# Prompt attention: the causal mask added by VectorE, the turn of probabilities as a product with diagonals

## The chip, the cores and the metric

One core of one Trainium2 chip runs the whole kernel. Its engines are TensorE (PE; its weight loads are shown apart as PEld), VectorE (DVE), ScalarE (ACT), GpSimd (POOL) and SyncE (SP), which issues most loads and stores. The metric is the device time of one execution in microseconds, over three runs.

## The reference, cut to what matters

The kernel computes one step of a hybrid decoder layer for a prompt of 512 rows and for 8 sequences of 4 new rows. The part that matters here is the prompt's attention over selected blocks and over the window. With 512 rows there are only 8 blocks and 16 may be chosen, so both branches become ordinary causal attention over 512 rows, each with its own keys and values:

```python
s_s = jnp.einsum('bqgrd,bqgkcd->bqgrkc', q, kb).astype(jnp.float32) * scale
m_s = (pos <= t_q[None, :, None, None, None]) & jnp.isfinite(top_s)[..., None]
p_s = masked_softmax(...)                      # selected branch
s_w = jnp.einsum('bqgrd,bkgd->bqgrk', q, kw).astype(jnp.float32) * scale
m_w = ((diff >= 0) & (diff <= WINDOW) & (t_w >= 0)[None, :])[None, :, None, None, :]
p_w = masked_softmax(s_w, m_w)                 # window branch
return gate[..., 0:1] * o_c + gate[..., 1:2] * o_s + gate[..., 2:3] * o_w
```

There are 2 groups of 6 query heads with 64 numbers each. A row's probabilities are the exponentials over their sum, and each branch's output is scaled by a gate of that row, head and branch.

## The kernel before, in words

The kernel goes through its stages one after the other: input projections, the RWKV scan, a stretch of "fill" projections that run beneath the scan and the compressed attention, then the prompt's attention, the prompt's memory attention, the same for the samples, the merge and the feed-forward part. The order on each engine is written out by hand; engines meet through semaphores. No planner sets the order in the stretch of the change.

Prompt attention is cut into units, `ATT_UNITS`. A unit is (r, t, bs): the query head r of both groups (g = 0, 1), the tile t of 128 query rows, and the branches bs. For t = 0 and 1 both branches fit a unit; for t = 2 and 3 there is one unit for each branch. So a head has 6 units (t = 0, 1, 2, 2, 3, 3), and 6 heads have 36. Only keys up to the tile's end are used, w = (t + 1) x 128 of them, so the mask matters in the last 128 keys alone.

A unit passes these steps:

- `att_scores` (TensorE, L1733): q times keys into the accumulator `acc[u % 2]`, one product per group, in f32 with 64 rows of weights. Then, at L1735, one bf16 product per group of the identity with the causal mask (0 or -1e30) adds the mask to the last 128 keys of each branch. From the third unit on it first waits for the exponentials of the unit two before (`at_exp`). It counts up `at_s`.
- `att_max` (VectorE, L3017) waits for `at_s` and takes the negated maximum over each row.
- `att_exp` (ScalarE, L2396) writes exp(score - maximum) to `probs[u % 3]` and the sums to `small`.
- `att_scale` (VectorE): reciprocal of the sums (L3027), times the gate (L3028), then the probabilities times that factor, in place: one tensor_tensor where a unit has two branches (L3032), one tensor_scalar per group where it has one (L3035). It counts up `at_scaled`.
- `att_turn` (TensorE, L1745) waits for `at_scaled` and transposes each 128x128 block of `probs` into `acc[2]`: 4, 8, 6, 6, 8 and 8 blocks in the six units of a head, 40 in all.
- `att_copy` (ScalarE, L2406) copies them to `probsT`.
- `att_values` (TensorE, L1756) multiplies them with the values into `acc[3]`, with 64 columns of weights per group. After a head, `att_out` (VectorE, L3041) adds the result to `onsaT`.

TensorE's loop is scores(u), turn(u - 2), values(u - 3). VectorE's is max(u), scale(u - 1), and now and then `att_out`. ScalarE's is copy(u - 2), exp(u). `settle()` is a count of TensorE's own semaphore between groups. `own(...)` on VectorE runs an instruction and then waits until it is done.

Behind the 36 units comes the prompt's memory attention, with scores (L1769), transposes of 128x128 blocks (L1796, eight for a query tile) and values (L1809, eight f32 products of 128x128 weights with 128 columns for a query tile).

The buffer that the change adds lies in the region `late_at`, where the fill stretch kept rows on their way to memory; each store counts up a semaphore `spilled`. SyncE waits for all of them before it issues the page keys (L730) of the third pair of samples.

Of the kernel before, what the change touches and what calls it, by code (L numbers as in the profile page):

```python
# [13 lines left out]
P = 128  # L14
# [230 lines left out]
def bc(ap, axis, n):  # L245

    a = ap.unsqueeze(axis)
    shape = list(a.shape)
    shape[axis] = n
    return a.to_broadcast(shape)  # L250
# [17 lines left out]
def program(nc, A):  # L268
    with ExitStack() as ctx:
# [21 lines left out]
        def region(start, *shape):  # L291

            if start is None:
                start = at[0]
            n = int(np.prod(shape))
            at[0] = start + n
            assert at[0] <= 35200, at[0]
            ap = work[:, KT * T + start:KT * T + start + n]
            names = "abcd"[:len(shape)]
            if len(shape) == 1:  # L300
                return ap
            return ap.rearrange(f"p ({' '.join(names)}) -> p {' '.join(names)}",
                                **dict(zip(names[1:], shape[1:])))

        def const(name, rows=P):
            lo, hi = SEG[name]
            return cst[0:rows, lo:hi]
# [21 lines left out]
        bf_causal = region(None, P // 2).bitcast(BF16)  # L329
        bf_cmp = region(None, QT * NC_P // 2).bitcast(BF16)  # L330
        late_at = at[0]
        m_probT = [region(None, MEM_H * 2, P) for _ in range(2)]
        assert at[0] <= 16800
        smp1 = 16800
        w1_two = region(smp1 + 7168, 2, CMP // 2, P)
# [699 lines left out]
        def _(pe):  # L1035
# [687 lines left out]
            def att_scores(u):  # L1723
                r, t, bs = ATT_UNITS[u]
                w, nb = (t + 1) * P, len(bs)
                if u >= 2:
                    pe.wait_ge(at_exp, u - 1)
                settle()
                o = acc[u % 2][:, :, 0:nb * w].rearrange("p g (b k) -> p g b k", b=nb)
                for g in range(NG):  # L1730
                    gs = slice(g * HD, (g + 1) * HD)
                    keys = in_all[gs, T_ATT[bs[0]]:T_ATT[bs[-1]] + 1:T_WK - T_SK, 0:w]
                    pe.matmul(o[:, g], qT[gs, r, t * P:w], keys, start=True, stop=False)  # L1733
                for g in range(NG):
                    mm = pe.matmul(o[:, g, :, t * P:w], bf_ident, bc(bf_causal, 1, nb), start=False, stop=True)  # L1735
                mm.then_inc(at_s, 1)

            def att_turn(u):
                r, t, bs = ATT_UNITS[u]
                pe.wait_ge(at_scaled, u + 1)  # L1740
                if u:
                    pe.wait_ge(at_copied, u)
                for g in range(NG):
                    for k in range(len(bs) * (t + 1)):
                        mm = pe.transpose(acc[2][:, g, k * P:(k + 1) * P], probs[u % 3][:, g, k * P:(k + 1) * P], ident)  # L1745
                mm.then_inc(at_turn, 1)

            def att_values(u):
# [844 lines left out]
        def _(dve):  # L2593
# [419 lines left out]
            def att_max(u):  # L3013
                r, t, bs = ATT_UNITS[u]
                w, nb, c = (t + 1) * P, len(bs), 16 * (u % 2)
                dve.wait_ge(at_s, u + 1)
                dve.tensor_reduce(small[:, c:c + 2 * nb].rearrange("p (g b) -> p g b", g=NG),  # L3017
                                  acc[u % 2][:, :, 0:nb * w].rearrange("p g (b k) -> p g b k", b=nb), AX, ALU.max, negate=True)\
                   .then_inc(at_max, 1)

            def att_scale(u):
                r, t, bs = ATT_UNITS[u]
                w, nb, c = (t + 1) * P, len(bs), 16 * (u % 2)
                rows = lambda n: small[:, c + n:c + n + NG * nb]
                gates = gates_tm[:, t, :].rearrange("p (g r b) -> p g r b", g=NG, b=3)[:, :, r, 1 + bs[0]:2 + bs[-1]]
                dve.wait_ge(at_exp, u + 1)
                own(dve.reciprocal(rows(8), rows(4)))  # L3027
                own(dve.tensor_tensor(rows(12).rearrange("p (g b) -> p g b", g=NG),  # L3028
                                      rows(8).rearrange("p (g b) -> p g b", g=NG), gates, ALU.mult))
                if nb == 2:  # L3030
                    shown = probs[u % 3][:, :, 0:nb * w].rearrange("p g (b k) -> p g b k", b=nb)
                    ins = dve.tensor_tensor(shown, shown, bc(rows(12).rearrange("p (g b) -> p g b", g=NG), 3, w), ALU.mult)  # L3032
                else:
                    for g in range(NG):
                        ins = dve.tensor_scalar(probs[u % 3][:, g, 0:w], probs[u % 3][:, g, 0:w],  # L3035
                                                small[:, c + 12 + g:c + 13 + g], None, ALU.mult)
                ins.then_inc(at_scaled, 1)

            def att_out(r):
                dve.wait_ge(at_pv, HEAD_UNITS * (r + 1))  # L3040
# [1 line left out]

            page_copy(0)
            att_max(0)
            for u in range(1, N_ATT + 1):
                if u < N_ATT:
                    att_max(u)
                if u == 1:
                    new_copy(0)
                att_scale(u - 1)  # L3050
                if u >= 5 and (u - 5) % HEAD_UNITS == HEAD_UNITS - 1:
                    att_out((u - 5) // HEAD_UNITS)
# [386 lines left out]
```

## Time and profile before

| | |
|---|---|
| median of 3 runs | 1466.07 us (1464.58 to 1468.4) |
| profiled execution | 1465.81 us, span 1464.1 us, mean granted clock 0.996 |
| TensorE busy | 1430.9 us, 98% of the span |
| VectorE, ScalarE, GpSimd busy | 847.9, 413.0 and 211.9 us |
| prompt attention's first scores | 665.74 us from the start of the span |
| its last values (L1756) start | 775.8 us |

The page gives busy times of the whole span; its ends of matmuls are modelled, so how tightly TensorE is packed is read from starts in the timeline. In a timeline row the numbers are the start and the length in us, then engine, line, operation, the program's names (written from read), the size of the weights, the shape of one operand and the count of merged instructions. In brackets is the idle time before, with its releaser. In a row of windows come: the window, its length, the busy time and count of PE, PEld, DVE, ACT and POOL, the granted clock as a share, the share of the DMA engines and GB/s. In a row of grouped instructions come: busy us in total, mean ns of one, and the idle time before.

### The profile page before, as it was taken

To read this page: it belongs to the slowest core of one execution; us is meant where nothing else is said; L and a number is where in the kernel's file an instruction comes from. 1 tells how busy PE (TensorE), PEld (TensorE's weight loads), DVE (VectorE), ACT (ScalarE), POOL (GpSimd) and SP (SyncE) were. 2 spreads that over 40 slices of the span, in tenths; PEclk is the share of its full clock that TensorE was granted. 3 is DMA by queue.
4 is the path that set the end of the run, shared out by engine and by line. 5 is a ranking of instruction groups with operands and counts; after the bars stand their busy time and mean duration, and the time that the engine had idled before them with its cause. 6 is when DMAs were issued, how large, how long until landed. Compare 5 with 4: busy or idle time off the path is not lost.

```text
span 1464.1 us, 30419 instructions
## 1 busy us (share of the span) xinstructions
PE 1430.9 (98%) x12340; PEld 1130.4 (77%) x12340; DVE 847.9 (58%) x1649; ACT 413.0 (28%) x890; POOL 211.9 (14%) x276
## 2 busy tenths in 40 slices
PE   9999999999999999999999889999999999999997
PEld 8887578878888866775667668888888888888886
DVE  7665058633433447526774537677666766666664
ACT  3112372123333316227775631102311011101001
POOL 1000324532222224434001210000000000000000
PEclk9999999999999999999999999999999999999999
DMA  6222543211111238457003963432222222222221
GB/s 264 87 87 72 182 166 111 96 61 44 50 46 36 101 118 254 156 165 250 1 2 91 334 260 137 141 98 83 75 84 86 76 83 87 87 74 97 90 87 61
DMA packets 57399, 163.94 MB, mean 112 GB/s; under 512 B 7312, under 2 KB 19696, under 8 KB 55952
## 3 DMA queue, kind: packets, MB, share of 16 engines
q1 hardware_dynamic: 48608, 121.46, 24.9%
q0 software_dynamic: 7936, 39.40, 7.8%
q8 instruction: 99, 1.62, 0.5%
q10 hardware_dynamic: 720, 1.16, 0.2%
q14 instruction: 36, 0.29, 0.1%
HBM read 144.01 MB, written 22.15 MB: 113 GB/s over the span
## 4 chain that ended last, share of the span: by engine, by line
PE 91%; DVE 4%; ACT 2%; issue 1%; SPq 1%; DMA 1%; DVEq 0%; ACTq 0%
PE acc L1059 26%; PE acc L1210 17%; PE acc L1978 5%; PE acc L2006 5%; PE acc L1987 5%; PE acc L2031 4%; PE acc L1152 2%; PE acc L1332 2%; PE acc L1167 2%; PE acc L1733 2%; PE acc L1745 2%; PE acc L1756 1%; PE acc L1349 1%; PE acc L1094 1%; PE acc L1071 1%
## 5 line engine op out<-in xcount | busy, mean ns | idle before, releaser
L1059 PE MATMUL acc<-sb_work,sb_ring 128*128 128x272 f32 x602 | 150.9, 392 | 0.0
L2524 ACT ACTIVATE sb_omemT<-acc 128x272 f32<-128x272 f32 x74 | 29.3, 396 | 386.0 <-PE acc L1978 234.2
L1210 PE MATMUL acc<-sb_work,sb_ring 128*128 128x272 f32 x504 | 129.2, 398 | 4.4 <-DVE sb_work L2733 2.9
L1059 PE MATMUL acc<-sb_work 128*128 128x272 f32 x530 | 133.0, 393 | 0.0
L1059 PEld LDWEIGHTS acc<-sb_work,sb_ring 128*128 128x128 f32 x602 | 114.4, 190 | 23.6
L1059 PEld LDWEIGHTS acc<-sb_work 128*128 128x128 f32 x530 | 100.5, 190 | 21.4 <-issue 0.8
L1210 PEld LDWEIGHTS acc<-sb_work,sb_ring 128*128 128x128 f32 x504 | 93.1, 190 | 25.7 <-issue 7.1
L1978 PE MATMUL acc<-sb_work,sb_ring 128*128 128x272 f32 x308 | 77.2, 393 | 1.0 <-issue 1.0
L1987 PE MATMUL acc<-sb_work,sb_ring 128*128 128x272 f32 x308 | 77.1, 392 | 0.0
L1210 PE MATMUL acc<-sb_onsaT,sb_omemT 128*128 128x272 f32 x272 | 69.5, 399 | 0.0
L1978 PEld LDWEIGHTS acc<-sb_work,sb_ring 128*128 128x128 f32 x308 | 58.4, 190 | 13.4 <-issue 1.4
L1987 PEld LDWEIGHTS acc<-sb_work,sb_ring 128*128 128x128 f32 x308 | 58.5, 190 | 12.1
L1059 PE MATMUL acc<-sb_onsaT,sb_work 128*128 128x272 f32 x266 | 66.6, 393 | 0.0
L1059 PE MATMUL acc<-sb_onsaT,sb_ring 128*128 128x272 f32 x266 | 66.5, 392 | 0.0
L1210 PEld LDWEIGHTS acc<-sb_onsaT,sb_omemT 128*128 128x128 f32 x272 | 50.2, 190 | 13.3 <-issue 3.2
L1059 PEld LDWEIGHTS acc<-sb_onsaT,sb_work 128*128 128x128 f32 x266 | 50.4, 190 | 10.6 <-issue 0.2
L1059 PEld LDWEIGHTS acc<-sb_onsaT,sb_ring 128*128 128x128 f32 x266 | 50.5, 190 | 10.4
L2830 DVE TENSOR_TENSOR sb_work<-acc,sb_cst 128x192 f32<-128x192 f32 x64 | 22.7, 358 | 55.8 <-PE acc L1332 55.5
L1210 PE MATMUL acc<-sb_work,sb_omemT 128*128 128x272 f32 x208 | 53.8, 399 | 0.0
L3017 DVE TENSOR_REDUCE sb_small<-acc 128x2 f32<-128x768 f32 (+3 forms) x36 | 37.7, 1047 | 20.4 <-PE acc L1735 19.6
L844 POOL TENSOR_TENSOR sb_omemT<-sb_ring 128x512 f32<-128x512 f32 x20 | 26.1, 1304 | 148.7 <-PE acc L1210 100.8
L1210 PEld LDWEIGHTS acc<-sb_work,sb_omemT 128*128 128x128 f32 x208 | 38.3, 190 | 9.8 <-issue 1.2
(495 smaller groups left out, 2787.4 us busy)
## 6 DMA issues: line engine op xcount, KB each, us to landing
sb_ring<-w_stream SPq DMA_DIRECT2D x144, 512.0 KB, 3.5
sb_work<-pages SPq DMA_DIRECT2D x56, 192.0 KB, 4.2
branch_gates<-sb_work SPq DMA_DIRECT2D x24, 272.0 KB, 2.8
sb_work<-branch_gates POOLq DMA_DIRECT2D x8, 816.0 KB, 14.7
sb_ring<-w_stream SPq DMA_DIRECT2D x16, 384.0 KB, 3.3
sb_work<-mem_kT SPq DMA_DIRECT2D x8, 512.0 KB, 7.5
sb_work<-mem_v SPq DMA_DIRECT2D x8, 512.0 KB, 9.9
query_features<-sb_work SPq DMA_DIRECT2D x10, 272.0 KB, 3.5
```

What stands on the lines that cost most here:

```text
L1059: mm = pe.matmul(out, w[:, q, :], x[q], start=q == 0, stop=q == n - 1)
L1152: mm = pe.matmul(acc[n][:, h, :], memT[:, k, n * P:(n + 1) * P], w[:, 4 * h:4 * h + 4, :].rearrange("p a c -> p (a c)"), start=k == 0, sto ...
L1167: mm = pe.matmul(acc[a][:, b, 0:HALF_T], lhsT, rhs[:, b * HALF_T:(b + 1) * HALF_T], start=True, stop=True)
L1210: mm = pe.matmul(acc[3][:, (7 * u + ph) % 2, 0:HALF_T], w, x, start=q == 0 and ph in (0, 1, 5), stop=q == 3, skip_group_check=True)
L1332: mm = pe.matmul(acc[1][rows[1 - e], s, k * C:k * C + n], gram[rows[e], par, e, 3 * s + k, n:2 * n], X(par, 3 * s + k)[rows[e], 0:n], star ...
L1733: pe.matmul(o[:, g], qT[gs, r, t * P:w], keys, start=True, stop=False)
L1978: mm = pe.matmul(bank(u, 0), w[:, 2 * q, :], x[:, x0 + 2 * q, LO], start=q == 0, stop=q == n - 1)
L1987: mm = pe.matmul(bank(u, 1), w[:, 2 * q + 1, :], x[:, x0 + 2 * q + 1, LO], start=q == 0, stop=q == n - 1)
L2006: mm = pe.matmul(bank(u, 3), s1[:, q, :], sums[:, 0, q], start=q == 0, stop=q == n - 1)
L2031: mm = pe.matmul(acc[out][:, b, 0:HALF_T], w[:, k, :], sources[g][:, k, b * HALF_T:(b + 1) * HALF_T], start=k == 0, stop=k == MERGE_KS[g] - 1)
L2524: act.activation(keeps(u)[:, s], bank(u, (0, 3)[s]), ACT.Copy).then_inc(unit_kept, 1)
L3017: dve.tensor_reduce(small[:, c:c + 2 * nb].rearrange("p (g b) -> p g b", g=NG), acc[u % 2][:, :, 0:nb * w].rearrange("p g (b k) -> p g b k ...
```

## The change

Three things are changed.

1. `att_scores` no longer adds the mask. `att_max` does it on VectorE: one tensor_tensor per unit adds the f32 constant "causal" to the last 128 keys of each group and branch, in place in the accumulator, and waits for its own end before the maximum.
2. `att_scale` no longer scales the probabilities. It builds, for each group and branch, a 128x128 diagonal matrix: the identity times the factor gate over sum of each row (`scale_diag`, three buffers in turn). `att_turn` multiplies each block of raw exponentials with that diagonal instead of transposing it against the identity. A block as weights times a diagonal gives the transposed block with its columns scaled.
3. `scale_diag` gets the place of the two `m_probT` buffers, which now lie over it, and VectorE waits, after the first unit's maximum, for all `spilled` counts.

```diff
@@ buffers
         late_at = at[0]
-        m_probT = [region(None, MEM_H * 2, P) for _ in range(2)]
+        scale_diag = region(late_at, 3, 2 * NG, P)
+        m_probT = [region(late_at + n * MEM_H * 2 * P, MEM_H * 2, P) for n in range(2)]
@@ att_scores
-                    pe.matmul(o[:, g], qT[gs, r, t * P:w], keys, start=True, stop=False)
-                for g in range(NG):
-                    mm = pe.matmul(o[:, g, :, t * P:w], bf_ident, bc(bf_causal, 1, nb), start=False, stop=True)
+                    mm = pe.matmul(o[:, g], qT[gs, r, t * P:w], keys, start=True, stop=True)
                 mm.then_inc(at_s, 1)
@@ att_turn
-                        mm = pe.transpose(acc[2][:, g, k * P:(k + 1) * P], probs[u % 3][:, g, k * P:(k + 1) * P], ident)
+                        mm = pe.matmul(acc[2][:, g, k * P:(k + 1) * P], probs[u % 3][:, g, k * P:(k + 1) * P],
+                                       scale_diag[:, u % 3, g * len(bs) + k // (t + 1), :], start=True, stop=True)
@@ att_max
                 dve.wait_ge(at_s, u + 1)
+                ahead = acc[u % 2][:, :, 0:nb * w].rearrange("p g (b k) -> p g b k", b=nb)[:, :, :, t * P:w]
+                own(dve.tensor_tensor(ahead, ahead, bc(bc(const("causal"), 1, nb), 1, NG), ALU.add))
@@ att_scale
-                if nb == 2:
-                    shown = probs[u % 3][:, :, 0:nb * w].rearrange("p g (b k) -> p g b k", b=nb)
-                    ins = dve.tensor_tensor(shown, shown, bc(rows(12).rearrange("p (g b) -> p g b", g=NG), 3, w), ALU.mult)
-                else:
-                    for g in range(NG):
-                        ins = dve.tensor_scalar(probs[u % 3][:, g, 0:w], probs[u % 3][:, g, 0:w],
-                                                small[:, c + 12 + g:c + 13 + g], None, ALU.mult)
-                ins.then_inc(at_scaled, 1)
+                dve.tensor_tensor(scale_diag[:, u % 3, 0:NG * nb, :], bc(ident, 1, NG * nb), bc(rows(12), 2, P), ALU.mult)\
+                   .then_inc(at_scaled, 1)
@@ VectorE's attention loop
             att_max(0)
+            for n in range(2):
+                dve.wait_ge(spilled[n], 16 * N_FILL // 2)
```

## Rows read from the trace of the kernel before

**Rows 1.** The page: busy time, granted clock in 40 slices, chain that ended last.

```profile
PE 1430.9 (98%) x12340; PEld 1130.4 (77%) x12340; DVE 847.9 (58%) x1649; ACT 413.0 (28%) x890; POOL 211.9 (14%) x276
...
PEclk9999999999999999999999999999999999999999
...
PE 91%; DVE 4%; ACT 2%; issue 1%; SPq 1%; DMA 1%; DVEq 0%; ACTq 0%
```

**Rows 2.** One head in a window: length, busy (count) of five engines, clock, DMA, GB/s.

```profile
680.00:697.29 17.29, 17.17 (x158) 10.98 (x158) 13.49 (x30) 13.33 (x38) 7.16 (x13) 1.00 0.82 254
```

**Rows 3.** Timeline of one head: start, length (us), engine, line, operation, idle before.

```profile
680.00 0.88 PE L1756 MATMUL acc<-sb_work 128*64 128x128 f32 x12
...
680.81 0.70 PE L1733 MATMUL acc<-sb_work 64*128 64x256 f32 x4
...
680.97 0.88 DVE L3035 TENSOR_SCALAR sb_omemT<-sb_omemT,sb_small 128x512 f32<-128x512 f32 x2
...
681.44 0.39 PE L1735 MATMUL acc<-sb_work 128*128 128x256 bf16 x2
...
681.91 0.86 PEld L1745 LDWEIGHTS acc<-sb_cst,sb_omemT 128*128 128x128 f32 x8 [0.35 <-DVE sb_omemT L3035]
...
683.74 1.13 PE L1733 MATMUL acc<-sb_work 64*128 64x512 f32 x4
...
684.81 0.39 PE L1735 MATMUL acc<-sb_work 128*128 128x256 bf16 x2
...
685.03 1.04 PE L1745 MATMUL acc<-sb_cst,sb_work 128*128 128x128 f32 x8
...
685.24 1.23 DVE L3017 TENSOR_REDUCE sb_small<-acc 128x4 f32<-128x1024 f32 x1 [1.48 <-PE acc L1735]
...
686.00 1.10 PE L1756 MATMUL acc<-sb_work 128*64 128x128 f32 x16
...
686.38 0.17 DVE L3027 RECIPROCAL sb_small<-sb_small 128x4 f32<-128x4 f32 x1
...
686.78 0.69 DVE L3032 TENSOR_TENSOR sb_omemT<-sb_omemT,sb_small 128x512 f32<-128x512 f32 x1
...
687.88 0.29 PE L1735 MATMUL acc<-sb_work 128*128 128x128 bf16 x2
...
688.01 0.61 PE L1745 MATMUL acc<-sb_cst,sb_omemT 128*128 128x128 f32 x4
...
688.54 1.10 PE L1756 MATMUL acc<-sb_work 128*64 128x128 f32 x16
...
690.76 0.86 PEld L1745 LDWEIGHTS acc<-sb_cst,sb_omemT 128*128 128x128 f32 x8 [0.22 <-DVE sb_omemT L3032]
```

**Rows 4.** Groups of instructions by shape: the mask matmuls of two-branch units.

```profile
L1735 PE MATMUL acc<-sb_work 128*128 128x256 bf16 x24 | 4.7, 278 | 0.0
```

**Rows 5.** Timeline of TensorE in the memory attention that follows.

```profile
777.79 1.04 PE L1796 MATMUL acc<-sb_cst,sb_work 128*128 128x128 f32 x8
...
778.67 1.89 PE L1769 MATMUL acc<-sb_work 128*128 128x256 f32 x8
...
780.40 1.95 PE L1809 MATMUL acc<-sb_work 128*128 128x128 f32 x16
...
782.18 1.04 PE L1796 MATMUL acc<-sb_cst,sb_work 128*128 128x128 f32 x8
```

**Rows 6.** VectorE groups with PSUM input: from the page, and from the groups by shape.

```profile
L2830 DVE TENSOR_TENSOR sb_work<-acc,sb_cst 128x192 f32<-128x192 f32 x64 | 22.7, 358 | 55.8 <-PE acc L1332 55.5
...
L3041 DVE TENSOR_TENSOR sb_onsaT<-acc,sb_onsaT 128x512 f32<-128x512 f32 x6 | 4.1, 686 | 0.6 <-PE acc L1756 0.6
```

**Rows 7.** Timeline at the start of attention: first scores, second unit's turn.

```profile
665.74 0.70 PE L1733 MATMUL acc<-sb_work 64*128 64x256 f32 x4
...
673.47 1.09 PE L1745 MATMUL acc<-sb_cst,sb_omemT 128*128 128x128 f32 x8 [0.44 <-DVE sb_omemT L3032]
```

**Rows 8.** Timeline of SyncE's queue: its first load behind the wait for the spills.

```profile
661.36 3.97 SPq L730 DMA_DIRECT2D sb_work<-pages  x8
```

## The prediction

> **What bounds the kernel.** I read the page first. TensorE (PE) is busy 98% of the span, the clock is granted at its higher level (2.4 GHz) in all 40 slices, and PE holds 91% of the chain that ended last [rows 1]. So a microsecond put on PE in the changed stretch is a microsecond at the end, unless PE waits there for somebody else. Next I cut prompt attention into heads. One head is six units of the pipeline; its window of 17.29 us has PE busy for 17.17 but VectorE for only 13.49 and ScalarE for 13.33 [rows 2]; four more heads give the same to 0.02 us. PE's busy time is modelled, so I checked it by starts in the timeline. Each group starts where the one before hands over: scores at 683.74, mask at 684.81, turn at 685.03, values at 686.00 [rows 3]. Only two turns in six start late. The mask at 681.44 takes 0.22, as at 684.81 to 685.03, so the turn could start at 681.66 and does at 681.91; the turn at 690.76 stands 0.22 on its weight load, of which I count 0.20. Both times the releaser is VectorE's scaling of the probabilities. That is 0.25 + 0.20 = 0.45 us of real waiting in a head; the other 16.8 us are PE's own work.
>
> **Mask off PE.** By starts a mask costs 0.22 us in the units with two branches (684.81 to 685.03) and 0.13 in those with one (687.88 to 688.01) [rows 3]. There are 24/2 = 12 of the first [rows 4] and, of 36 units, 24 of the second: 12 x 0.22 + 24 x 0.13 = 5.8 us, all on PE's path. The busy time of such a group, 4.7 us for the first kind, is no measure: it holds the tail of the last matmul, which overlaps the next group.
>
> **Turn as a product.** The same blocks, 4 + 8 + 6 + 6 + 8 + 8 = 40 in a head and 240 in all, go through the array, now as f32 products of 128x128 weights with 128 columns. The trace has this product: the memory attention's values (L1809). It issues 8 products there and the timeline counts 16 matmuls; 8 turns (L1796) count 8. By starts, 16 matmuls take 780.40 to 782.18 = 1.78 us, and 8 turns 777.79 to 778.67 = 0.88 [rows 5]. So a product goes as two matmuls of 0.111 us, a turn as one of 0.110, and a block gets dearer by 0.90/8 = 0.1125 us. A head pays 40 x 0.1125 = 4.5 us, all six 27.0. Bounds: at the 0.107 us per matmul that the weight-load side shows for turns (0.86/8 [rows 3]) a block adds 0.105 (25 us); with the whole 1.95 us of that row over 16, 0.122 a matmul, it adds 0.134 (32 us), but the tail is in that, so I keep 27.
>
> A rule speaks against this edit. The Trainium skill (Perfetto Trace Analysis, section Transposes) says that a logical transpose should use the transpose and not a standard matmul. It gives no factor; the trace agrees, with 0.88 us against 1.78 for eight blocks.
>
> **VectorE.** Added: one add into PSUM per unit, over 512 elements a partition in two-branch units and 256 in the others. The trace has no tensor_tensor that writes PSUM; reading PSUM, 192 elements take 0.358 us and 512 take 0.686 [rows 6]. Between them 256 gives 0.42. I take 0.42 and 0.69, with about 0.05 us for the wait on its own semaphore (reciprocal at 686.38 with 0.17, next but one at 686.78: steps of 0.20 [rows 3]). Bounds for the small one are those two rows; for a surcharge of the PSUM write, 0 and, as a doubling of the larger row, 0.69. The diagonals: the same 512 or 256 elements in SBUF, 0.69 (686.78 [rows 3]) or 0.42. Removed: scaling of 512 and 1024 elements in the two-branch units (0.69, and 1.23 by the reduction of equal size), and two-instruction pairs in the four others, of which the long ones take 0.88 by the union (680.97 [rows 3]). I take 0.8 on average for all four. Per head: +3.06 for adds, +3.06 for diagonals, +0.3 for waits, -5.1 for scaling: about +1.3, so VectorE has 13.5 + 1.3 = 14.8 us in a head. PE will have 20.4 (below). VectorE isn't the bound; 5.6 us are spare.
>
> **Does the round trip still fit?** Turn(u-2) stands behind scores(u) and needs VectorE's add and reduction of u-1 and then its small operations and diagonals of u-2. Take the last unit of a head, where scores start at time 0. They end at 1.13 (683.74 [rows 3]) and VectorE starts 0.04 later, at 1.17. Add 0.42 + 0.05, reduction 1.23, then reciprocal and product of the gates 0.4 less an overlap of 0.09, diagonals 0.42: 3.60, and 0.05 to PE. PE meanwhile does scores 1.07 (683.74 to 684.81), a turn of 6 blocks, values 0.81 (680.00 to 680.81), the next scores 0.63 (680.81 to 681.44). Turns of 8 and 4 blocks take 0.97 and 0.53 by starts (685.03 to 686.00, 688.01 to 688.54 [rows 3]), so one of 6 takes 0.75 now and 0.75 + 6 x 0.1125 = 1.42 then. Together 3.93. Slack 0.28. For the second unit's turn, the other late one, the same working gives 0.25. So the new add is hidden by the longer turns, and the 0.45 us of waiting in a head goes too. If this cover were gone, each 0.1 us past the slack costs 0.1 us, twice a head. ScalarE's load is unchanged at 13.3 of 20.4. Behind VectorE's waiting add stand the reduction and the scaling of the unit before, and for these wait ScalarE's exponentials and PE's turn; they are in this working.
>
> **Start.** The second unit's turn already waits there for VectorE (0.44 us at 673.47 [rows 7]). The adds of the first three units now lie on this chain, 0.74 + 0.74 + 0.47; against that the scores are ready 0.2 to 0.4 earlier, VectorE has gaps between them, and 1.23 of scaling becomes 0.69. By laying these out I get turn(1) 0.6 us later than now (bounds: 0, and 1.95 with all three adds and nothing back). Its wait absorbs what the first turn and the first four masks (0.7) changed, so behind it count 236 blocks, 5.8 - 0.7 = 5.1 of masks, and 5 x 0.45 = 2.25 of waits.
>
> **Nothing for:** the new wait for the spilled fill rows. SyncE waits for the same count and goes on at 661.36 [rows 8], while the first scores start at 665.74 [rows 7]; if that cover went, VectorE and all behind it would stand for the difference. Nothing too for the moved buffers of the turned memory probabilities: same sizes, same operations, written after the last turn. No DMA is added or moved. Behind attention the loads wait for the end of the memory attention and shift with it.
>
> **Sum.** +0.6 + 236 x 0.1125 (26.55) - 5.1 - 2.25 = +19.8 us. As a check, a head becomes 17.28 + 4.5 - 0.97 - 0.45 = 20.36. The profiled execution took 1465.81 us around its span of 1464.1, so it becomes 1485.6; it lies 0.26 under the median of the runs shown, 1466.07. Forecast: 1485.9.
>
> **Rivals.**
> 1. *Round trip late again.* A write into PSUM, or its semaphore, costs more than the 0.25 to 0.28 us of slack, so PE waits at two to four turns of six. For: VectorE released late turns before, and no row prices the write. Against: slack in every unit. With 0.2 to 0.5 us at two or three turns over six heads, 2.4 to 9 us more: 1488 to 1495. Chance 0.14.
> 2. *The other side: a product with a diagonal costs PE no more than a turn* (one matmul per block, or the second hides in gaps). It decides at an extra of (5.1 + 2.25 - 0.6)/236 = 0.029 us per block; below that the change isn't slower. At nothing extra: 1466.1 + 0.6 - 5.1 - 2.25 = 1459.3. For: ends on PE are modelled, and nothing but starts prices the second matmul. Against: the counts, 16 for 8, and the starts [rows 5]; a diagonal is nothing to the array but 128 columns. Chance 0.03.
> 3. *A product takes four times a turn.* Its mechanism would be that only the turn passes the array without arithmetic, and f32 products of probabilities pay four passes of 0.11: 0.44 a block, 0.33 more than now, and 236 x 0.33 = 78 replace the 26.55: 1537. For: turns are a form of their own. Against: L1809 has the same shape and type and takes 0.22 [rows 5]. Chance 0.01. The Trainium skill (TensorE: Matmul & The Clock Gate, section Terms) calls the transpose mode 4x faster for FP32; the rows show a factor of two.
> 4. *Part comes back behind attention* (loads that land late now would be hidden). PE holds 91% of the chain [rows 1], so little can: 3 to 8 us, 1478 to 1483. Chance 0.06.
>
> **Chances.** The forecast has 0.76. Its own range, with 25 to 28 us for the blocks and 0 to 1.95 for the start, is 1483 to 1488. The range for 8 in 10 takes in the nearer halves of rivals 1 and 4: 1479 to 1492. A measurement of this kernel tells 0.3% (4.4 us) from no change; slower by more holds for all but rival 2: slower 0.96, same 0.01, faster 0.03.
>
> **What would show it.** In the changed profile the mask's matmuls are gone; the turns show 480 matmuls, not 240; a head's window is 20.2 to 20.6 us; starts of a turn of eight blocks to its values lie 1.8 to 1.9 us apart, not 0.97; no turn in the steady heads waits for VectorE; VectorE's busy time in a head is near 14.5. A head above 21 us with VectorE as the turns' releaser is rival 1; one near 16 us is rival 2. A head of 20.4 with a total more than 3 us off 1486 would put my error outside attention.

## The result, and the profile after

The changed kernel took 1486.21 us in the median of four runs (1485.47 to 1487.79); the kernel before took 1465.32 beside it. The ratio is 1.0143, with a 95% interval of 1.0121 to 1.0166. It is slower, by 20.9 us of medians, and 0.3 us from the forecast of 1485.9.

The page of the kernel after, the lines that answer to [rows 1]:

```profile
PE 1451.8 (98%) x12508; PEld 1157.3 (78%) x12508; DVE 853.3 (58%) x1661; ACT 412.9 (28%) x890; POOL 211.3 (14%) x276
...
PEclk9999999999999999999999999999999999999999
...
PE 92%; DVE 3%; ACT 1%; issue 1%; DMA 1%; SPq 1%; DVEq 0%; ACTq 0%
```

TensorE (PE) is as full as before, 21 us busier, and holds 92% of the chain where it held 91. The 40 slices hide what the clock did; the windows below don't. They are the start of attention in two pieces, then one head (the columns are those of [rows 2]):

```profile
666.00:671.30 5.30, 2.66 (x36) 1.16 (x35) 4.60 (x10) 3.85 (x16) 2.14 (x4) 1.00 0.88 287
671.30:674.80 3.50, 3.40 (x13) 2.13 (x13) 2.19 (x5) 2.44 (x9) 2.13 (x4) 0.54 1.00 353
684.48:705.40 20.92, 20.92 (x187) 15.47 (x185) 14.52 (x32) 13.42 (x39) 4.44 (x9) 1.00 0.51 168
```

A head takes 20.92 us where it took 17.29 [rows 2], and PE is busy for all of it. VectorE has 14.5 us of work in it, ScalarE 13.4. Before this head, the first microseconds of attention have PE idle for half of 5.3 us, and then a mean granted clock of 0.54 of full speed: the lower level, 1.2 GHz, for nearly all of that window.

One unit of a head in the timeline of the kernel after, the answer to [rows 3]:

```profile
687.90 1.13 PE L1734 MATMUL acc<-sb_work 64*128 64x512 f32 x4
...
688.96 1.86 PEld L1744 LDWEIGHTS acc<-sb_work 128*128 128x128 f32 x16 [0.76 <-issue]
688.96 2.05 PE L1744 MATMUL acc<-sb_work 128*128 128x128 f32 x16
...
689.08 0.70 DVE L3018 TENSOR_TENSOR acc<-acc,sb_cst 128x512 f32<-128x512 f32 x1 [1.70 <-PE acc L1734]
...
689.81 1.22 DVE L3019 TENSOR_REDUCE sb_small<-acc 128x4 f32<-128x1024 f32 x1
...
690.95 1.10 PE L1756 MATMUL acc<-sb_work 128*64 128x128 f32 x16
690.96 0.17 DVE L3029 RECIPROCAL sb_small<-sb_small 128x4 f32<-128x4 f32 x1
...
691.35 0.69 DVE L3032 TENSOR_TENSOR sb_work<-sb_cst,sb_small 128x512 f32<-128x512 f32 x1
```

No mask stands between scores and turn. The turn of eight blocks shows 16 matmuls, from 688.96 to the values at 690.95: 1.99 us by starts, where [rows 3] had 0.97. VectorE adds the mask in 0.70 us, 0.03 after that the reduction starts, and the diagonals end at 692.04, so at 692.83 the turn that needs them finds them ready. The start of attention, the answer to [rows 7]:

```profile
665.82 1.56 PE L1734 MATMUL acc<-sb_work 64*128 64x256 f32 x8
...
669.67 0.92 PE L1734 MATMUL acc<-sb_work 64*128 64x384 f32 x4 [1.93 <-ACT sb_omemT L2396]
...
671.40 1.86 PE L1744 MATMUL acc<-sb_work,sb_omemT 128*128 128x128 f32 x8 [0.81 <-DVE sb_work L3032]
...
673.19 1.65 PE L1734 MATMUL acc<-sb_work 64*128 64x384 f32 x4
...
674.77 2.15 PE L1744 MATMUL acc<-sb_work,sb_omemT 128*128 128x128 f32 x16
...
676.85 0.66 PE L1756 MATMUL acc<-sb_work 128*64 128x128 f32 x8
```

TensorE stands 1.93 us before the third unit's scores and 0.81 before the first turn; the scores at 673.19 take 1.65 us where those at 669.67 took 0.92.

To see where 19.7 us of span went I took the starts of the same steps in both traces. Each number is the time in us between the first matmuls of two steps:

| stage | before | after | difference |
|---|---|---|---|
| attention, first scores to first memory scores | 101.50 | 123.26 | +21.8 |
| memory attention, to the second pair's compression | 24.91 | 26.74 | +1.8 |
| samples, to the last memory rows | 43.21 | 43.10 | -0.1 |
| samples' values, to the merge | 28.00 | 22.87 | -5.1 |
| merge to the end | 600.78 | 602.07 | +1.3 |

The second stage holds the last two turns of eight blocks. So the edit cost 23.6 us in attention, 3.8 more than the 19.8 of my sum, and 3.9 us came back behind it, in code that the edit doesn't touch. The forecast was near because two errors cancelled, and that was luck. In the samples' values TensorE of the kernel before stands at two places "on issue", for nothing that the profile shows, and at half clock behind the second:

```profile
839.13 1.03 PE L1820 MATMUL acc<-sb_cst,sb_work 128*128 128x128 f32 x8 [1.46 <-issue]
...
845.48 0.44 PE L1840 MATMUL acc<-sb_ring,sb_work 128*32 128x64 f32 x8 [3.51 <-issue]
```

```profile
842.00:845.50 3.50, 0.02 (x3) 0.02 (x3) 0.00 (x0) 1.62 (x4) 0.00 (x0) 0.94 0.65 236
845.50:848.00 2.50, 2.50 (x40) 1.38 (x44) 0.89 (x2) 0.44 (x2) 0.00 (x0) 0.50 0.19 34
848.00:850.00 2.00, 2.00 (x20) 0.59 (x12) 0.00 (x0) 0.13 (x2) 0.00 (x0) 0.50 0.99 335
```

In the kernel after it stands at other matmuls, for less, and the clock stays high (the windows lie behind the first and behind the second):

```profile
864.75 0.88 PE L1840 MATMUL acc<-sb_ring,sb_work 128*32 128x64 f32 x48 [1.41 <-issue]
...
869.65 0.49 PE L1840 MATMUL acc<-sb_work 128*32 128x64 f32 x18 [1.09 <-issue]
```

```profile
866.00:868.00 2.00, 2.00 (x48) 1.07 (x48) 0.97 (x3) 1.62 (x5) 0.00 (x0) 1.00 1.05 352
870.00:873.00 3.00, 3.00 (x74) 2.57 (x66) 1.42 (x4) 0.86 (x1) 0.00 (x0) 1.00 0.34 84
```

### The profile page after: what moved, and what is told of

It reads as the page before. It is cut to its first block, busy times and chain, and to the rows that moved or that the text cites. A ratio compares the mean times of both kernels' runs of the same rounds, so it can differ in the third digit from the quotient of the medians.

```text
span 1483.8 us, 30768 instructions
## 1 busy us (share of the span) xinstructions
PE 1451.8 (98%) x12508; PEld 1157.3 (78%) x12508; DVE 853.3 (58%) x1661; ACT 412.9 (28%) x890; POOL 211.3 (14%) x276
## 3 DMA queue, kind: packets, MB, share of 16 engines
q1 hardware_dynamic: 48608, 121.46, 24.8%
## 4 chain that ended last, share of the span: by engine, by line
PE 92%; DVE 3%; ACT 1%; issue 1%; DMA 1%; SPq 1%; DVEq 0%; ACTq 0%
PE acc L1060 26%; PE acc L1211 16%; PE acc L2006 5%; PE acc L1978 5%; PE acc L1987 5%; PE acc L1744 4%; PE acc L2031 2%; PE acc L1734 2%; PE acc L1756 2%; PE acc L1153 2%; PE acc L1333 2%; PE acc L1168 2%; PE acc L1350 1%; PE acc L1095 1%; PE acc L1072 1%
## 5 line engine op out<-in xcount | busy, mean ns | idle before, releaser
L1060 PEld LDWEIGHTS acc<-sb_work,sb_ring 128*128 128x128 f32 x602 | 114.4, 190 | 23.6
L1978 PEld LDWEIGHTS acc<-sb_work,sb_ring 128*128 128x128 f32 x308 | 58.4, 190 | 13.4 <-issue 1.4
L1744 PEld LDWEIGHTS acc<-sb_work,sb_omemT 128*128 128x128 f32 x312 | 37.4, 194 | 14.2 <-issue 11.4
L1211 PEld LDWEIGHTS acc<-sb_work,sb_omemT 128*128 128x128 f32 x208 | 38.3, 190 | 10.0 <-issue 1.2
```

The source lines that it names most:

```text
L1060: mm = pe.matmul(out, w[:, q, :], x[q], start=q == 0, stop=q == n - 1)
L1211: mm = pe.matmul(acc[3][:, (7 * u + ph) % 2, 0:HALF_T], w, x, start=q == 0 and ph in (0, 1, 5), stop=q == 3, skip_group_check=True)
L1744: mm = pe.matmul(acc[2][:, g, k * P:(k + 1) * P], probs[u % 3][:, g, k * P:(k + 1) * P], scale_diag[:, u % 3, g * len(bs) + k // (t + 1), ...
L1978: mm = pe.matmul(bank(u, 0), w[:, 2 * q, :], x[:, x0 + 2 * q, LO], start=q == 0, stop=q == n - 1)
```

## The experiments

I numbered TensorE's records (weight loads, matmuls and its own semaphore instructions) in the order of time in each trace; a number is good to one or two, since weight loads run ahead of matmuls. The two gaps stand 256 records apart in both kernels, at 19138 and 19394 before, at 19650 and 19906 after: multiples of 256 plus 194, all four. The page of the kernel before gives the third number of this kind:

```profile
q8 instruction: 99, 1.62, 0.5%
```

99 transfers of instructions for 25,387 records of TensorE are one for every 256, of 1.62 MB / 99 = 16 KB each. In all 13 kernels of this document this queue's count is TensorE's records over 256, rounded down: from 98 for 25,243 to 101 for 25,899. The change removes 144 records (mask) and adds 480 (second weight load and matmul of each block): +336, which is 80 modulo 256. A gap at a fixed record number then falls 80 records earlier in the work, or 176 later; from the start of the last sample pair's turns (L1820, at 837.23 us before and 860.77 after) the second gap lies 262 records on before and 437 after, 175 more. This gave the experiments a second question beside the parts of the edit.

### First set: the parts alone

To keep these boundaries in place I put idle instructions (counts of TensorE's own semaphore) among the warm-up matmuls at the program's start. That was a bad tool: attention started 22 to 23 us later in the two runs with 144 of them, 8.7 later with 80, 3.7 later with 32. Not all of it is theirs. At the matmul that stands 12 us from the start in the kernel before, the delay was 18.3, 6.7 and 0.5 us; the remainder arose between there and attention: some of it at gaps of the kind above and, with 144, in 3.4 us of half clock at 315 us, some with no cause shown. The totals of these four runs hold the whole delay; the lengths of the stages from attention on don't.

**The mask alone** (`e1_mask_only`), with 144 idle instructions:

```diff
-                    pe.matmul(o[:, g], qT[gs, r, t * P:w], keys, start=True, stop=False)
-                for g in range(NG):
-                    mm = pe.matmul(o[:, g, :, t * P:w], bf_ident, bc(bf_causal, 1, nb), start=False, stop=True)
+                    mm = pe.matmul(o[:, g], qT[gs, r, t * P:w], keys, start=True, stop=True)
@@ att_max
+                ahead = acc[u % 2][:, :, 0:nb * w].rearrange("p g (b k) -> p g b k", b=nb)[:, :, :, t * P:w]
+                own(dve.tensor_tensor(ahead, ahead, bc(bc(const("causal"), 1, nb), 1, NG), ALU.add))
```

> The kernel before with the mask alone moved to VectorE (turn and scaling as before). TensorE's program would be 144 instructions shorter, so 144 counting instructions that do nothing stand among its first matmuls: the boundaries of 256 instructions stay where they were. Theory (the mask's 0.97 us per head come off TensorE but VectorE is now late): a head of VectorE is adds 3.1, reductions 6.3, small operations 2.1, scaling 5.3, att_out 0.7 and some gaps, 17.7 to 18.3 us against 17.28, so the heads give +2.5 to +6 us, the start 1 to 3 more; about 1470, with VectorE as the turns' releaser in most units. Rival (TensorE bounds here too): a head of 16.3 to 16.8 us and 1460 to 1463.

Measured: 1493.67 us, ratio 1.0174 (1.0152 to 1.0196). The total was missed: 22.8 us of it lie ahead of attention. A head takes 17.91 us, in the expected range. One turn of a head, and VectorE's scaling before it:

```profile
760.52 0.88 DVE L3038 TENSOR_SCALAR sb_omemT<-sb_omemT,sb_small 128x512 f32<-128x512 f32 x2
...
761.32 0.69 DVE L3019 TENSOR_TENSOR acc<-acc,sb_cst 128x512 f32<-128x512 f32 x1
...
761.46 1.10 PE L1746 MATMUL acc<-sb_cst,sb_omemT 128*128 128x128 f32 x8 [1.06 <-DVE sb_omemT L3038]
...
762.48 0.88 PE L1757 MATMUL acc<-sb_work 128*64 128x128 f32 x12
```

TensorE waits 1.06 us for the scaling. The theory held: without the longer turns VectorE is late, and the mask's move alone costs 0.6 us a head. It also shows the turn of transposes directly behind scores: 761.46 to 762.48, 1.02 us against the 0.97 of [rows 3], where a mask product stood ahead of it.

**The diagonals alone** (`e2_diagonal_only`), with the mask as before, 32 idle instructions, and the changed kernel's `att_scale`:

```diff
-                        mm = pe.transpose(acc[2][:, g, k * P:(k + 1) * P], probs[u % 3][:, g, k * P:(k + 1) * P], ident)
+                        mm = pe.matmul(acc[2][:, g, k * P:(k + 1) * P], probs[u % 3][:, g, k * P:(k + 1) * P],
+                                       scale_diag[:, u % 3, g * len(bs) + k // (t + 1), :], start=True, stop=True)
```

> The kernel before with the product with diagonals alone (the mask stays a bf16 product on TensorE); 32 idle instructions keep TensorE's code boundaries where they were. Theory (a turn costs TensorE 0.11 us per matmul plus 0.22 fixed, of which 0.10 is an entry behind scores with 64 rows of weights, which the mask pays here instead): turn of eight blocks to values 1.88 us, a head 21.3 to 21.4, heads +24.4 us; 1490. Rival (only 0.1125 per block as I predicted, mask removal worth its full 0.97 in the changed kernel): a head 17.28 + 4.5 - 0.45 = 21.33 too, but a turn of eight blocks to values of 1.98, and the changed kernel's 20.92 stays unexplained.

Measured: 1493.61 us, ratio 1.0192 (1.0174 to 1.021), 3.6 us over the expected total, with attention 3.7 us late. A head takes 21.48 us.

```profile
708.57 0.39 PE L1739 MATMUL acc<-sb_work 128*128 128x256 bf16 x2
708.80 1.95 PE L1749 MATMUL acc<-sb_work,sb_omemT 128*128 128x128 f32 x16
710.68 0.88 PE L1761 MATMUL acc<-sb_work 128*64 128x128 f32 x12
```

The turn of eight blocks takes 708.80 to 710.68, 1.88 us, against 1.98 in the changed kernel. So a product behind scores with 64 rows of weights pays 0.10 us to get in, and where the mask of a two-branch unit stands between, the mask pays it. Behind the shorter mask of a one-branch unit about half of it stays: there turns of 8, 6 and 4 blocks take 1.93, 1.49 and 1.04 us, against 1.98, 1.53 and 1.09 in the changed kernel. The Trainium skill (TensorEngine Tiling (Array Packing), section Key Properties) says that changing the tiling mode drains TensorE; these starts agree, with 0.10 us for the product and 0.05 for the transposes. The diagonals alone cost attention and memory attention 24.8 us, the mask alone 5.4 (6.8 us of half clock at its start are in that), both together 23.6: the longer turns cover VectorE's adds, and the mask's departure then pays 0.56 us a head (21.48 to 20.92), not 0.97.

**The turn as a transpose in the changed kernel** (`e3_turn_without_scaling`), the mask on VectorE, 144 idle instructions at the start; its output leaves out the scaling by gate over sum:

```diff
-                        mm = pe.matmul(acc[2][:, g, k * P:(k + 1) * P], probs[u % 3][:, g, k * P:(k + 1) * P],
-                                       scale_diag[:, u % 3, g * len(bs) + k // (t + 1), :], start=True, stop=True)
+                        mm = pe.transpose(acc[2][:, g, k * P:(k + 1) * P], probs[u % 3][:, g, k * P:(k + 1) * P], ident)
```

> The changed kernel with the turn as a transpose of the raw exponentials; the diagonals are still built but not used, so the scaling by gate over sum is left out. 144 idle instructions keep TensorE's code boundaries of the kernel before. Theory (the product is what costs): a head of 16.3 to 16.9 us, that is 4.0 to 4.6 under the changed kernel's 20.92, and about 1462. Rival (the mask's and the diagonals' place on VectorE costs the time): a head stays above 17.3 and the total above 1466.

Measured: 1484.75 us, ratio 1.0114 (1.0094 to 1.0135), with attention 21.9 us late. A head takes 16.69 us, 4.23 less than 20.92, and attention 99.62 in place of 123.26. With the total I was wrong, because of what lies ahead of attention; the head is in the range. The product is the whole cost: without it attention is 1.9 us shorter than before the change.

**The kernel before with shifted code** (`e4_before_shifted_code`):

```diff
-            keep_clock(20)
+            for k in range(20):
+                keep_clock(1)
+                for _ in range(4 + (k < 0)):
+                    settle()
```

> The kernel before, with 80 idle instructions among TensorE's first matmuls and nothing else. The changed kernel has 336 more TensorE instructions in attention, which is 80 modulo 256. Theory (TensorE's two gaps in the samples' stage, 1.5 and 3.5 us with a half clock behind the second, stand at boundaries of 256 instructions, where the next 16 KB of code come late behind a full DMA): the gaps move to 176 instructions later, as in the changed kernel, cost 2.5 us instead of 5 and leave the clock high: about 5 us faster, 1460 to 1461. Rival (the gaps belong to the work or its data): they stay at the same matmuls and the time is 1465.

Measured: 1472.49 us, ratio 1.0045 (1.0027 to 1.0062): slower, not 5 us faster. 8.7 us lie ahead of attention. Attention is the same to 0.01 us; the samples' values take 22.86 us in place of 28.00, and the gaps stand where the changed kernel has them:

```profile
849.11 0.88 PE L1843 MATMUL acc<-sb_ring,sb_work 128*32 128x64 f32 x48 [1.14 <-issue]
...
854.29 0.49 PE L1843 MATMUL acc<-sb_work 128*32 128x64 f32 x18 [1.36 <-issue]
```

The place was right, the total was missed. Of the 8.7 us, 1.2 are a new gap in the scan, at record 11714, another multiple of 256 plus 194.

### Second set

**The first two masks on TensorE** (`e5_first_masks_on_pe`), in the changed kernel:

```diff
-                    mm = pe.matmul(o[:, g], qT[gs, r, t * P:w], keys, start=True, stop=True)
+                    mm = pe.matmul(o[:, g], qT[gs, r, t * P:w], keys, start=True, stop=u >= 2)
+                if u < 2:
+                    for g in range(NG):
+                        mm = pe.matmul(o[:, g, :, t * P:w], bf_ident, bc(bf_causal, 1, nb), start=False, stop=True)
```

and on VectorE the add stands under `if u >= 2`.

> The changed kernel, but the first two units keep their mask on TensorE and VectorE adds none for them (8 instructions more on TensorE). Theory (the start of attention lost time because the adds stood before the first exponentials, TensorE idled 1.9 and 0.8 us and its clock was then granted at half for 3.4 us): the gap before the third unit's scores goes back to 0.6, the clock stays high at the start, and the first head is 1.2 to 2.5 us shorter than 18.66, later heads stay at 20.92; total 1484 to 1485. Rival (the clock or the gap has another cause): the first head stays above 18.3.

Measured: 1485.29 us, ratio 1.0122 (1.0107 to 1.0138). The gap before the third unit's scores went back to 0.66, as in the kernel before, the one before the first turn was 0.96 (0.81 in the changed kernel), and the clock still fell for 3.4 us. The first head took 18.40. The part about the gap held, the part about the clock didn't.

**The kernel before with smaller warm-up products** (`e6_before_smaller_warmup`), which shifts the code by 80 without idle instructions:

```diff
-                    pe.matmul(acc[0][:, 0, 0:P], ones_h, ones_h, start=True, stop=True)
+                    pe.matmul(acc[0][0:HD, 0, 0:HD], ones_h[:, 0:HD], ones_h[:, 0:HD], start=True, stop=True)
-            keep_clock(20)
+            keep_clock(40)
```

> The kernel before, with its 20 warm-up products of 128x128 at the start made 40 of 64x64: 160 instructions in place of 80, so TensorE's code behind them stands 80 later modulo 256, without the idle instructions of the earlier try, which cost 8.7 us ahead of attention. Theory (late code at boundaries of 256 instructions): the samples' stage (from the third memory rows to the merge) takes 22.9 us in place of 28.0, the gaps are 1.1 and 1.4 us, the clock stays high there, and the total is 1460 to 1463 if the start costs nothing. Rival: 28.0 us there and 1465 to 1466.

Measured over five rounds: 1464.98 us, ratio 0.9986 (0.9977 to 0.9995). The samples' values take 22.87 us, as expected. But attention starts 3.4 us later: 0.7 from the warm-up, and 2.7 in the scan, where a gap of 1.35 us opened at record 11714, as in `e4_before_shifted_code`. The shift moves every gap of this kind, not only the two that I had looked at, so the net is 2 us.

**The exponentials and diagonals in bf16** (`e7_bf16_turn`), sums and values' products still in f32:

```diff
-        probs = [om[:, n * 2 * TP:(n + 1) * 2 * TP].rearrange("p (g k) -> p g k", g=2) for n in range(2)] + [region(PROB_AT, 2, TP)]
+        probs = [om[:, n * 2 * TP:n * 2 * TP + TP].bitcast(BF16).rearrange("p (g k) -> p g k", g=2) for n in range(2)]\
+            + [region(PROB_AT, TP).bitcast(BF16).rearrange("p (g k) -> p g k", g=2)]
-        scale_diag = region(late_at, 3, 2 * NG, P)
+        scale_diag = region(late_at, 3 * NG * P).bitcast(BF16).rearrange("p (n b t) -> p n b t", n=3, b=2 * NG)
```

> The changed kernel with exponentials and diagonals in bf16, so the turn's product is bf16; sums, maxima and the values' products stay f32. Theory (an f32 product goes as two matmuls of 0.11 us and that is the cost of the change): a block goes as one matmul of 0.055 to 0.06, a turn of eight blocks to values takes 0.65 to 0.75 us in place of 1.98, and VectorE (14 us and its gaps) becomes the bound with a head of 15.0 to 16.3; total 1453 to 1460. Rival (the fixed part of a turn is what costs): a head above 17.3.

Measured: 1456.08 us, ratio 0.993 (0.9915 to 0.9945): faster than the kernel before. A head takes 15.63 us.

```profile
728.84 0.42 DVE L3033 TENSOR_TENSOR sb_work<-sb_cst,sb_small 128x256 bf16<-128x256 f32 x1
...
729.18 0.69 DVE L3019 TENSOR_TENSOR acc<-acc,sb_cst 128x512 f32<-128x512 f32 x1
...
729.32 0.62 PE L1745 MATMUL acc<-sb_work,sb_omemT 128*128 128x128 bf16 x8 [0.97 <-DVE sb_work L3033]
...
729.87 0.88 PE L1757 MATMUL acc<-sb_work 128*64 128x128 f32 x12
```

Eight blocks are eight matmuls, 0.55 us by starts (less than the expected 0.65), and TensorE has waited 0.97 us for the diagonals, which it does once a head. The cost was the f32 product's two matmuls, and with it gone the way through VectorE sets the head: VectorE is busy for 14.25 of the 15.64 us from 698.05, TensorE for 13.97.

**The changed kernel shifted back** (`e8_changed_shifted_back`), with the small products of `e6_before_smaller_warmup`:

```diff
-            keep_clock(20)
+            keep_clock(64)
```

> The changed kernel with 64 warm-up products of 64x64 in place of 20 of 128x128: 176 instructions more, which with its own 336 is 512, so the boundaries of 256 stand at the work as in the kernel before. Theory: the samples' stage takes 26.5 to 28 us in place of 22.9 and the kernel is 3.5 to 5 us slower than the changed one, 1490 to 1491, if the start costs nothing. Rival (the 5 us given back came from other timing in that stage): 22.9 us there.

Measured: 1493.73 us, ratio 1.0186 (1.017 to 1.0201). Attention starts 5.3 us later, so the total lies over the expected one. The gaps are back at the matmuls of the kernel before:

```profile
867.55 1.03 PE L1820 MATMUL acc<-sb_cst,sb_work 128*128 128x128 f32 x8 [1.73 <-issue]
...
873.90 0.32 PE L1840 MATMUL acc<-sb_ring,sb_work 128*32 128x64 f32 x8 [3.51 <-issue]
```

```profile
874.00:877.00 3.00, 3.00 (x48) 1.51 (x52) 0.89 (x2) 0.56 (x2) 0.00 (x0) 0.56 0.41 108
```

and so is the half clock behind the second. The samples' values take 27.06 us, 4.2 more than in the changed kernel, and the stretch from the merge to the end takes 600.77 in place of 602.07: the +1.3 of the last stage goes with the place of the code too.

### Third set

**The bf16 turn with the mask left on TensorE** (`e9_bf16_turn_mask_on_pe`): the kernel before with the edit of the diagonals alone and the bf16 edit, both shown above.

> The bf16 turn as in the run before it, with the mask left where it was, a bf16 product on TensorE. TensorE's instruction count is that of the kernel before. Theory (with a bf16 turn VectorE bounds the heads at 15.63 us, and its adds are 3.1 us of that, while the mask costs TensorE under 1 us): a head of 14.3 to 14.9 us, TensorE bounds again, attention to the memory scores 86 to 90 us in place of 92.7, the samples' stage back at 27 to 28 us since the code boundaries are those of the kernel before; total about 5 us under or equal to the bf16 run with VectorE's mask: 1451 to 1456. Rival (ScalarE's 13.3 us and the round trip bound the heads as well): 15.2 us and more.

Measured: 1450.75 us, ratio 0.9902 (0.988 to 0.9923), faster than both kernels and at the foot of the expected range. A head takes 14.71 us, attention 86.98, and no turn waits.

```profile
726.85 1.13 PE L1735 MATMUL acc<-sb_work 64*128 64x512 f32 x4
727.91 0.39 PE L1737 MATMUL acc<-sb_work 128*128 128x256 bf16 x2
728.14 0.61 PE L1747 MATMUL acc<-sb_work 128*128 128x128 bf16 x8
728.68 1.10 PE L1759 MATMUL acc<-sb_work 128*64 128x128 f32 x16
```

One group hands over to the next, the turn in 0.54 us. The rule of the Trainium skill that spoke against the edit (Perfetto Trace Analysis, Transposes: transpose rather than a standard matmul) held here for f32, 1.88 us against 0.97; but a bf16 product that also scales takes 0.54, less than the f32 transpose. No run turned bf16 exponentials with plain transposes and scaled them apart, so how much of this gain is the type's and how much the folded scaling's is not shown.

**The same with the smaller warm-up** (`e10_same_with_smaller_warmup`), 40 small products in place of 20, the edit of the second set:

> The same as e9_bf16_turn_mask_on_pe, with 40 warm-up products of 64x64 in place of 20 of 128x128 (80 instructions more on TensorE). Theory: attention as in that run; the samples' stage 22.9 us instead of 28; 3.4 us more ahead of attention, as the same edit of the kernel before showed; in sum 1 to 2 us faster. Rival: no difference in the samples' stage.

Measured: 1450.83 us, ratio 0.9893 (0.9875 to 0.9911), no different from the run before it. The samples' values took 22.91 in place of 26.39 us, attention started 2.8 us later, and the clock fell at the start of attention, though the gaps there are the same to 0.01 us. The windows after these gaps, first of this kernel, then of the one before it:

```profile
676.30:679.70 3.40, 3.40 (x24) 2.06 (x22) 2.18 (x5) 2.32 (x6) 2.25 (x4) 0.50 0.47 142
```

```profile
673.50:677.00 3.50, 3.50 (x36) 1.81 (x34) 2.52 (x6) 3.22 (x9) 2.31 (x4) 1.00 0.50 164
```

**All masks of the first head on TensorE** (`e11_first_head_masks_on_pe`), `6` in place of `2` in the edit of the first two masks:

> The changed kernel with the mask of the first six units (the first head) on TensorE. With only two units kept, the clock still fell to half for 3.4 us at the start and the first head took 18.40 us. Theory (idle time of TensorE in the first five microseconds of attention is what lets the clock fall, and the third unit's missing mask product and the add ahead of its maximum are the rest of it): gaps of 0.55 and about 0.55 as in the kernel before, clock high, first head 17.0 to 17.6 as in the run with the diagonals alone (17.06). Rival: the fall comes with the f32 products themselves, first head 18.2 or more; the run with the diagonals alone speaks against it.

Measured: 1485.98 us, ratio 1.0131 (1.0109 to 1.0154). The gaps are 0.66 and 0.75, the clock stays high there, the first head takes 17.06 us where the changed kernel has 18.66, and attention 121.66 in place of 123.26. The total shows nothing of it: the samples' values take 24.91 us in place of 22.87, with gaps of 1.07 and 1.61 us at other matmuls, and behind the second the clock falls for 3.4 us. In `e5_first_masks_on_pe` a gap of 1.61 us stands at nearly the same work (the two kernels differ by 16 instructions ahead of it) and the clock stays high. First this kernel, then that one:

```profile
868.51 0.65 PE L1843 MATMUL acc<-sb_work 128*32 128x64 f32 x30 [1.61 <-issue]
...
869.30:872.70 3.40, 3.40 (x24) 3.07 (x26) 1.42 (x4) 0.00 (x0) 0.00 (x0) 0.50 0.24 63
```

```profile
870.55:873.50 2.95, 2.95 (x71) 2.60 (x71) 1.35 (x4) 0.42 (x1) 0.00 (x0) 1.00 0.27 57
```

So the length of the gap ahead of it doesn't tell whether the clock falls.

## Why the prediction was right, point by point

The total was met by luck: attention was 3.8 us dearer than the sum, and 3.9 us came back in stages that the sum left alone. The mechanism in attention was right.

- **TensorE bounds attention.** Right for the changed kernel, where it is busy for all of a head, and for the product alone, at 21.48. With the mask alone VectorE's late scaling set the head, at 17.91, as the prediction's sentence on the lost cover had warned.
- **A block gets dearer by 0.1125 us.** Right for the blocks: turns of 8 and 4 blocks take 1.98 and 1.09 us behind scores, 0.2225 a block, against 0.1075 for transposes (1.02 and 0.59 in the transposing variants), 0.115 more. What I left out is a fixed part. I took L1809's 16 matmuls [rows 5], whose neighbours have its array shape. In attention the turn goes in from scores of 64 rows, 0.10 us more that the mask had paid. (The way out into values of 64 columns costs about 0.10 before and after, so it is no part of the growth.) Against the 0.97, 0.75 and 0.53 of the prediction all turns of a head grew by 3 x 1.01 + 2 x 0.78 + 0.56 = 5.15 us, not 4.5. This is the term that was mis-sized: 20.92 a head against 20.36. (The 0.65 give 21.01; two of the old turns of eight had taken 1.02 and not 0.97.)
- **The mask off TensorE gives 5.8 us.** Right by starts, but its product had also paid for the change from 64 to 128 rows, and with the product behind it the mask's departure gave back 0.56 of 0.97 us a head.
- **VectorE's load and the round trip.** Right. The add into PSUM took 0.70 and 0.43 us and its wait 0.03; no surcharge. 14.5 us in a head, predicted 14.8, and no turn in the steady heads waits for it. The mask alone, with nothing to cover it, showed the late round trip of rival 1.
- **The start, +0.6 us.** Too low. The second unit's turn came 1.3 us later [rows 7]; the stretch at half clock, which the prediction didn't foresee, lies ahead of it and is in that. With the first head's masks on TensorE that head takes 1.6 us less.
- **Nothing behind attention changes.** Wrong: 3.9 us came back, the amount of rival 4 (3 to 8 us), but by another mechanism than its hidden loads. The longer code moved the places where TensorE stands, and with them a half clock. Shifting the code of either kernel moved them as counted, with attention itself unchanged: 5.1 us of the samples' values went in the kernel before, 4.2 came back in the changed one. Of the other 0.9 us no run shows the cause; the half clock lasts 3.4 us in the changed kernel shifted back and 6.8 in the kernel before.
- **The spilled rows' wait and the moved buffers cost nothing.** VectorE goes from the first unit's reduction to the second unit's add in 0.61 us (667.30 to 667.91) with no idle time beyond its own; nothing shows a wait.

What stays open: what a gap waits for, why it is 1.1 us at one boundary and 3.5 at another, and why the clock falls at the start of attention, or behind a gap of 1.61 us, in one kernel and not in another with the same gaps. That the gap is late code is inferred from its places and from the instruction transfers' size; no row shows the wait itself. Whether a bf16 turn as a plain transpose would do as well as the bf16 product was not run. A repeated trace of one and the same kernel was not taken.

## What to carry to other kernels

Price a replaced TensorE operation by the starts of neighbours that switch the array in the same way, going in and coming out, not by a run of its own kind. Before a transpose is made a product, count the matmuls: in f32 the product has two where the transpose has one, in bf16 one of half the length, and of the kernels run here only those with the bf16 turn were faster than the kernel before by more than 0.2%. And when code that was not edited moves by some microseconds, compare the stages' durations and count the instructions ahead of them before looking for a cause in the data.

## What the runs showed of the hardware that I had not expected

- All of TensorE's gaps "on issue" of over 1.0 us behind the first 30 us stand, in the 13 traces, within one record of a multiple of 256 plus 194; shorter ones of 0.71 and 0.98 us (at 302.2 and 1026.0 us in the kernel before) stay with their work instead. In the samples' values there are two in each kernel, of 0.96 to 3.51 us, with the DMA share of the gap at 0.36 to 1.06. In or behind each of the six of 2.96 us or more (the kernel before and five experiments) the clock fell to 1.2 GHz; behind the twenty of 0.96 to 1.89 us it stayed at 1.00, but for the one of 1.61 us in `e11_first_head_masks_on_pe`. The samples' values took 22.86 to 22.91 us with the code 80 records on and 26.0 to 28.0 with it where the kernel before has it; the two of 28.0 have 6.8 us of half clock, the others 3.4.
- An instruction that does nothing but count a semaphore is not free among warm-up matmuls: with 80 of them the first projection started at 13.70 us and with 144 at 23.62, in place of 7.86. With 144 of them 26 matmuls of that projection took 8.77 us where 40 took 9.36 in the kernel before.
- VectorE's tensor_tensor with its output in PSUM, 256 elements a partition, took 0.43 us, and 512 took 0.70, as with the output in SBUF (0.69).
